# Earlier banks for what stands behind a further pass, and unread products in TensorE's gaps

## What is computed

```
h = rms_norm(x, g) * (1 + scale) + shift          # adaLN, before each sub-layer
x = x + gate1 * mixer(h)
scores = softmax(h @ router_w)                    # 16 experts, 4 groups: best group, then its two best
out[token] = sum over its two experts e of gate[e] * ((silu(h @ w1[e]) * (h @ w3[e])) @ w2[e])
x = x + gate2 * out
```

## Time and profile before

| | |
|---|---|
| median of 3 runs | 1588.24 us (1586.63 to 1589.04) |
| the profiled execution | 1582.39 us, of which the span is 1580.6 |
| TensorE (PE) busy | 1473.4 us, 93% |
| VectorE (DVE) busy | 631.9 us, 40% |
| ScalarE (ACT) busy | 297.4 us, 19% |
| moved | 495.29 MB, mean 313 GB/s |
| chain that ended last | PE 77%, DMA 11%, DVE 6%, ACT 3%, issue 2% |
| further passes in the run | 5 |

### The profile page before, as it was taken

How to read it: one execution, slowest core, us unless ns; L and a number is a source line. 1 busy time by engine, 2 the same in 40 slices (tenths; PEclk the granted TensorE clock), 3 DMA queues, 4 the chain that set the end, 5 groups by cost and what they waited for, 6 DMA issues and landing times.

```text
span 1580.6 us, 21260 instructions
## 1 busy us (share of the span) xinstructions
PE 1473.4 (93%) x7790; PEld 712.1 (45%) x7791; DVE 631.9 (40%) x1845; ACT 297.4 (19%) x503; POOL 0.2 (0%) x4
## 2 busy tenths in 40 slices
PE   6999999997799999989999799997989999999996
PEld 3454555654244344344344355554344444344433
DVE  4445665333314322322333448745122333432333
ACT  4322222131010011010010247623010011011001
POOL 0000000000000000000000000000000000000000
PEclk9999999998999999999999899998999999999999
DMA  9538667762969999999996601435899999999992
GB/s 326 197 134 297 254 255 262 297 281 94 392 264 397 427 427 426 425 427 428 424 414 241 237 1 54 201 118 213 339 399 427 424 429 423 401 428 428 424 402 97
DMA packets 67711, 495.29 MB, mean 313 GB/s; under 512 B 4608, under 2 KB 21264, under 8 KB 28368
## 3 DMA queue, kind: packets, MB, share of 16 engines
q1 hardware_dynamic: 66048, 489.33, 76.0%
q10 hardware_dynamic: 1616, 5.33, 1.1%
HBM read 493.06 MB, written 1.58 MB: 313 GB/s over the span
## 4 chain that ended last, share of the span: by engine, by line
PE 77%; DMA 11%; DVE 6%; ACT 3%; issue 2%; ACTq 0%; DVEq 0%; SPq 0%
PE PS L846 75%; DMA halves<-in_moe_w 11%; PE PS L850 2%; DVE xc L1853 1%; ACT hT L580 0%; DVE misc L1671 0%; DVE halves L1671 0%; DVE halves L1662 0%; DVE halves L1664 0%; ACT hT L829 0%; DVE halves L1490 0%; DVE halves L1663 0%; ACT halves L640 0%; ACT halves L742 0%; ACT h L641 0%
## 5 line engine op out<-in xcount | busy, mean ns | idle before, releaser
L846 PE MATMUL PS<-halves,hT 128*64 128x512 f32 x3072 | 673.0, 597 | 15.2 <-DMA halves<-in_moe_w 12.6
L846 PEld LDWEIGHTS PS<-halves,hT 128*64 128x64 f32 x3072 | 218.1, 138 | 452.0 <-issue 430.4
L846 PE MATMUL PS<-hT,halves 128*128 128x384 f32 x640 | 216.4, 494 | 1.9 <-ACT hT L580 1.9
L846 PE MATMUL PS<-halves 128*32 128x512 f32 (+5 forms) x928 | 194.1, 509 | 1.8 <-ACT halves L543 0.7
L846 PEld LDWEIGHTS PS<-hT,halves 128*128 128x128 f32 x640 | 120.8, 192 | 99.1 <-issue 21.1
L1934 DVE COPY misc<-PS 64x512 f32<-64x512 f32 x32 | 21.9, 683 | 333.7 <-PE PS L846 333.7
L846 PEld LDWEIGHTS PS<-halves 128*128 128x128 f32 (+2 forms) x928 | 96.6, 158 | 85.2 <-issue 44.5
L1853 DVE SCALAR_TENSOR_TENSOR xc<-PS,MOD,xc 128x128 f32<-128x128 f32 x336 | 112.3, 409 | 13.8 <-PE PS L846 11.8
L846 PE MATMUL PS<-stack,h 128*128 128x128 f32 x768 | 98.4, 288 | 18.9 <-issue 9.9
L846 PEld LDWEIGHTS PS<-stack,h 128*128 128x128 f32 x768 | 94.0, 202 | 30.5 <-issue 26.3
L602 ACT ACTIVATE hT<-PS 128x512 f32<-128x512 f32 x32 | 19.1, 597 | 430.7 <-PE PS L846 430.7
(11 more groups left out here) (234 smaller groups left out, 972.2 us busy)
## 6 DMA issues: line engine op xcount, KB each, us to landing
halves<-in_moe_w SPq DMA_DIRECT2D x192, 2048.0 KB, 17.7
halves<-in_ada_w SPq DMA_DIRECT2D x48, 1024.0 KB, 6.5
halves<-in_hy_w_in SPq DMA_DIRECT2D x12, 1024.0 KB, 5.1
halves<-in_rg_w_in SPq DMA_DIRECT2D x4, 2048.0 KB, 19.1
halves<-in_hy_w_out SPq DMA_DIRECT2D x4, 1024.0 KB, 9.4
halves<-in_rg_w_out SPq DMA_DIRECT2D x2, 2048.0 KB, 9.6
halves<-in_rg_wa SPq DMA_DIRECT2D x1, 2048.0 KB, 8.3
halves<-in_rg_wx SPq DMA_DIRECT2D x1, 2048.0 KB, 10.9
```

Source lines behind the costliest of these rows:

```text
L846: return nc.tensor.matmul(out, lhsT, rhs, start=start, stop=stop)
```

## The change

It has four parts.

- X_COMBINE is in another order: the banks come as 0, 2, 6, 4, 5, 7, 3, 1 instead of 6, 4, 0, 5, 7, 1, 2, 3. The channel blocks keep theirs.
- In a further pass the transposes of the gate matrix move from behind the gather to behind the w3 products, and ScalarE's copy of them from ahead of the copy of the tokens to behind the sigmoid.
- A helper `spin(n)` issues n products of 128x512 into a bank that nobody reads in that state. It is called at the start and twice in `mixer0`, around `norm_spread` in every norm, twice in `router` (before the wait for `rt_mask` and before the wait for `tok`), and in the r = 0 turn of the first group of each expert layer, behind a new `If(group < 1)` and a wait for bank 0.
- VectorE's first instruction zeroes RG, which the spins of the start and of `mixer0` multiply; the others multiply the identity by VT.

```diff
@@ TensorE
+            def spin(n, source=None, bank=0):
+                rows = VT[:, :, :].rearrange("p a b -> p (a b)") if source is None else source
+                for _ in range(n):
+                    mm(PS[:, bank, :], ident if source is None else source[:, 0:P], rows, True, True)
+
+            pe.wait_ge(S("spin_rows"), 1)
+            spin(2, RG)
             pe.wait_ge(S("f_in"), 16)
             mm(PS[0:64, 1, 0:N], f_w1, features, True, True).then_inc(S("f_mm"), 1)
...
             def norm(tag):
                 norm_sums(tag)
+                if tag == 1:
+                    pe.wait_ge(S("v_in"), 16)
+                spin(1, bank=3)
                 norm_spread(tag)
+                spin(2, bank=3)
...
             def mixer0():
+                spin(4, RG)
                 pe.wait_ge(S("f_sin"), 1)
                 mm(PS[:, 1, 0:N], f_w2, f_h1, True, True).then_inc(S("f_mm"), 1)
+                spin(5, RG)
                 pe.wait_ge(S("w3_in"), 32)
...
                     token_tile(l, i)
+                spin(5)
                 pe.wait_ge(S("rt_mask"), before("rt_mask", l) + 1)
...
                 last.then_inc(S("rt_mm"), 1)
+                spin(3)
                 pe.wait_ge(S("tok"), before("tok", l + 1))
@@ extra_pass
                     gather(l, 0, 4, Xpick, width).then_inc(S("x_G_mm"), 1)
-                    for t in range(NT):
-                        last = tr(PS[:, 7, P * t:P * t + P], Xgpick[:, t, :])
-                    last.then_inc(S("x_gpT_mm"), 1)
                     pe.wait_ge(S("x_xg"), n + 1)
...
                         last.then_inc(S(done_sem), 1)
+                    for t in range(NT):
+                        last = tr(PS[:, 7, P * t:P * t + P], Xgpick[:, t, :])
+                    last.then_inc(S("x_gpT_mm"), 1)
                     pe.wait_ge(S("x_hid"), n + 1)
@@ expert_layer, r = 0
                         else:
                             with pe.If(group > 0):
                                 spread(l, group, done + extra, 0, 4)
+                            with pe.If(group < 1):
+                                passed(done + extra, 0)
+                                spin(2)
                         pe.wait_ge(S("hid"), before("hid", l) + e + 1)
                         passed(done + extra, 2)
@@ ScalarE, further pass
-                                act.wait_ge(S("x_gpT_mm"), n + 1)
-                                a.activation(XgpT, PS[:, 7, 0:N], ACT.Copy).then_inc(S("x_gpT"), 1)
                                 act.wait_ge(S("x_xT_mm"), n + 1)
...
                                 a.activation(Xhid, PS[:, 4, 0:256], ACT.Sigmoid).then_inc(S("x_sig"), 1)
+                                act.wait_ge(S("x_gpT_mm"), n + 1)
+                                a.activation(XgpT, PS[:, 7, 0:N], ACT.Copy).then_inc(S("x_gpT"), 1)
@@ VectorE
+            v.memset(RG, 0.0).then_inc(S("spin_rows"), 1)
             link(v.memset(cT[:, :, :], 0.0))
@@
-X_COMBINE = ((0, 6), (2, 4), (4, 0), (6, 5), (1, 7), (3, 1), (5, 2), (7, 3))
+X_COMBINE = ((0, 0), (2, 2), (4, 6), (6, 4), (1, 5), (3, 7), (5, 3), (7, 1))
```

## The result

The kernel before takes 1587.43 us (median; 1585.67 to 1589.04). The changed kernel's median is 1565.11 over four executions, of which three took 1562.67 to 1565.42 and one 4025.51, for which nothing on record gives a reason and which the ratio leaves out; the median of the three is 1564.80. The ratio is 0.9864, 95% interval 0.9844 to 0.9884. The profiled execution took 1562.67, the one of before 1582.39, so those two traces must account for 19.7 us.

The account below looks back on a forecast made before the run. TensorE bounds nearly throughout, the weight stream each expert layer from its last restart. Terms 1.2 + 1.7 + 1.9 + 2.2 + 4.4 + 0 + 1.3 + 1.1 - 0.2 = 13.6 us, giving 1574.6 us; range 1568 to 1583.

Parts of the forecast that it names:

- opening, norm and routers: Spins there keep the clock up: opening 1.2 us, layer 1's first norm 1.7, the two routers 1.9 and 2.2.
- Rival 3: Spins don't keep the clock and make routers and opening late: 8.5 us slower, 1597; chance 0.07.
- Pass of expert 0: Layer 0, group 0: transposes and w2 products start sooner with the clock up; 4.4 us, between 0.5 and 4.6.
- Passes of expert 2 and of group 6: Expert 2: w2 starts where it did, 0; group 6: token products get bank 0 first, 1.3 us.
- Rival 1: The further passes' gains are taken by the stream or first-turn code loading: gain 6.8 us, 1581; chance 0.14.
- Pass of expert 15: Gate transposes still wait for bank 3, seventh; w2 starts at 883.2, not 884.34: 1.1 us, between 0 and 2.6.
- the new code moves these places: TensorE's code waits of 1.73 and 2.21 us in the loop's first turn, behind expert 0's pass, get moved.
- 0 for the later walks past it: The new If(group < 1), walked past in seven turns of each layer, costs 0 there.
- what it gains inside the full stretches is lost: Both expert layers: TensorE's gains while the weight stream is full count nothing; it then waits for weights.
- layer 1's lies within the full stream, so nothing in it counts: Layer 1's one further pass stands inside the full weight stream, so its gain is 0.
- the same 432 us: Layer 1's full stream keeps its length of 432 us but begins some 14 us sooner.
- Rival 2: Loop code is loaded again in later turns; chance 0.06.

Follow-up runs that it names:

- the second profile: The changed kernel run again unchanged for another profile: 1564.38 us, ratio 0.9861 to the kernel before.
- the kernel with more code: Changed kernel plus 24 unread products of 16 columns in layer 0's router, before the rank product: 1570.79 us, ratio 0.9896.
- the other kernel of the kind: Changed kernel without the eleven unread products of the opening and without the zeroing of RG: 1663.54 us, ratio 1.0484.

## Why the prediction was wrong in its size and right in most of its parts

With every term at its own upper bound the forecast's sum is 17.1 us. The measured 22 (19.7 between the profiles) needed something that the sum held at nothing.

- **Spins hold the clock: right in routers and norm, by luck or not at all in the opening.** Forecast 7.0 for opening, norm and routers, measured 6.7 as the difference to the 16-column spins, the two in the loop included. The forecast's lengths of spins are multiples of 0.87 us, a sixth of the 5.2 us between the first of the filter products at 59.04 and the next stage's at 64.27, and it takes a spin at 0.50 as twice as long; measured are 4.46 us for five in the first trace and 7.04 in the second, most of them at 0.50. That the clock was low in the opening before was the author's estimate: the profile gives 1.00 there, and only the lengths of products and weight loads speak for it. Routers 1.5 and 2.4 by the timeline for 1.9 and 2.2 (the token products' own row shrinks by 1.88 in layer 0), layer 1's norm 1.6 for 1.7. The opening's 2.5 in the two profiles is half the luck of a transfer; by the run with narrow spins there it is 0.4 to 1.2, for 1.2. Rival 3 is refuted for the routers, the norms and the total: the clock stayed up across gaps of up to 1.3 us. In the opening it was seen in the second profile (the clock at 0.50 for 6.8 us, five spins in 7.04 us for 4.56, their follower 1.8 us late).
- **Pass of expert 0: right in size, partly by luck.** Forecast 4.4, measured 4.5 from the w1 products to the restart. The w2 products start 2.6 us sooner in this stage (402.85 for 409.45, on a time that runs 4.0 sooner; 0.25 later than worked out), and the clock that was at 0.50 up to 412.9 is up. But it now stands at 0.50 for 3.4 us from 427 on, behind the wait for instructions at 426, which costs about what it gave here. And 1.6 us of the 4.5 is the waits for instructions in this turn, 2.35 in all for 3.94: not the order, but the code's place. The order alone gave 2.7 in this stage, the added instructions alone 1.2.
- **Passes of expert 2 and of group 6: right**, with 0 and 1.3 for 0 and 1.3. Rival 1 is refuted: the passes' gain reached the end, 8.7 us with the order alone.
- **Pass of expert 15: mis-sized in the first profile.** Forecast 1.1, bounds 0 to 2.6, measured 3.1. The step was right that bank 3 sets when w2 starts, and one step of the combine earlier is what that gave (7.6 to 6.1 us behind the combine's start). The missing part is the clock, which fell here for 6.8 us before and didn't after. In seven further profiles with the new order and the added instructions (the changed kernel's second among them) it fell for 3.4 us, and the stage was worth 1.3 to 1.7. So the first profile's 3.1 is its own, and the forecast was nearly right.
- **The step that failed** is that the sum has no term for the waits for instructions in the loops' first turns. The forecast had read these rows (2.21 and 1.73) and knew that "the new code moves these places", but it asked only whether more code could make the kernel slower, in its rivals; the only number for code in the sum is the "0 for the later walks past it", which was right. 179 instructions more (21439 for 21260) moved the loops' code, which is loaded in blocks of 16,384 bytes, and the waits changed with it: 1.73 and 3.97 went. The added instructions alone, with the spins' work taken out, are worth 5.3 us (interval 1 to 7). In that kernel's trace 3.4 of 5.0 us lie in the two stages with the waits.
- **A second step hid the first: "what it gains inside the full stretches is lost", and "layer 1's lies within the full stream, so nothing in it counts".** The first holds for layer 0 (-0.4), and neither holds for layer 1, whose stretch was forecast at "the same 432 us" and took 429.0. There the stream was not full at three places. Behind the first turn's 8 us of waits it ran at 406 GB/s over 48 us, after the change at 424: 2.0 us. Behind layer 1's own further pass it fell to 252 GB/s, which the new order mended: 1.6 us. Near its end it lost 0.7 us more than before. That a single long wait costs little is shown by the kernel with more code, where 4.44 us are back and some 0.5 us is left of it at the end.
- **Rival 2**, with its chance of 0.06, stands for loop code that is loaded again in later turns. It isn't what happened here, but 44 instructions fewer on TensorE made it happen, and its price is about 100 us (1663.54 for 1564.38, 95 fetches for 32): the later turns of one layer pay, and the full stream doesn't hide it. It is a matter of place and not of size in the runs at hand: the loop of the kernel before, at its old length, paid 93 us once it was moved (31 fetches became 95).

Open: what decides whether layer 1's loop stays loaded, and why in layer 1 alone; how TensorE's waits turn into a dip of the stream (that its slots come back late fits the traces, but no run varies it alone); and what sets the third dip, which differs from kernel to kernel, so that the worth of each dip at the end of the run is less certain than its size.

## What to carry to other kernels

Look at the queue that loads instructions before and after any edit, even one of a few instructions far from a loop: if the count of its fetches jumps, or TensorE waits on "issue" in later turns of a loop, the edit's own effect can't be read until the loop has been moved (here 95 fetches for 32, 76.3 us of such waits in layer 1, 99 us in all), and an experiment that removes instructions needs a twin that keeps their number. Fill a gap with unread products only where the product behind it is on the path and its data comes later than they end; here 512 columns held the clock at 1.00 in the routers, and 16 columns left it at 0.50 for 3.4 us of the product behind. "Inside a full stream nothing counts" has to be checked in short stretches: a mean share of 1.00 over 432 us held places at 252 GB/s. Look for them behind the longest waits before taking a gain there as 0.

## What the runs showed of the hardware

- The same loop, moved by 27 narrow products (108 instructions) at the start of the kernel, cost 93 us: 95 fetches of 16,384 bytes for 31, and waits of up to 4.3 us (7.7 in the other kernel of the kind).
- The code of layer 0's loop stayed loaded from turn to turn in the kernel before: five fetches between 390 and 447 us, in its first turn, and none from there to 900. In layer 1's loop of the kernel without the opening's spins 59 fall between 1150 and 1620 us.
- Waits of TensorE for which the profile shows no releaser ended 2.5 to 2.9 us behind a fetch of 16,384 bytes, in all five cases of the kernel before.
- In some executions the clock fell to 0.50 while TensorE ran products of 32 output columns with hardly a gap (1.6 us into 24 records of them at 78.14), in others of the same kernel it didn't. With dense products put between them it stayed at 1.00 in the one profile taken, and five executions lay within 2.3 us.
- Products of 512 columns that nobody reads kept the granted clock at 1.00 through both routers, and products of zeros had the filter products behind them done in 5.39 us for 8.15 in the first trace; products of 16 columns in the routers did not hold it (0.50 from 365.4 to 368.8).
